# Causal scores in late columns and early quadrants, one weight split moved to GpSimd, and a half-width first level of the inverse

## The reference

```
S = S * w_t[:, :, None, :] + sa[..., None] * bb_t[:, :, None, :] + v_t[..., None] * k_t[:, :, None, :]
y_t = jnp.einsum('bhvk,bhk->bhv', S, r_t)     # sa = S @ aa_t, aa = -kk, bb = kk * a
```

## Time and profile before

| | us |
|---|---|
| median of 3 runs | 1025.52 |
| lowest, highest | 1024.86, 1025.6 |
| profiled execution: its own time | 1025.08 |
| profiled execution: span of its instructions | 1023.1 |

### The profile page before, as it was taken

How to read it: one execution, slowest core, us unless ns; L and a number is a source line. 1 busy time by engine, 2 the same in 40 slices (tenths; PEclk the granted TensorE clock), 3 DMA queues, 4 the chain that set the end, 5 groups by cost and what they waited for, 6 DMA issues and landing times.

```text
span 1023.1 us, 18706 instructions
## 1 busy us (share of the span) xinstructions
PE 1010.8 (99%) x7098; PEld 806.0 (79%) x7098; DVE 736.5 (72%) x1233; ACT 516.5 (50%) x869; POOL 218.1 (21%) x290
## 2 busy tenths in 40 slices
PE   8999999999999999999999999999999999999997
PEld 7888888777777777777777888888888888888886
DVE  5224667788988988888877455367777777789786
ACT  6435766844445445345453322265455444467744
POOL 8532356230221312313210454000000000000000
PEclk9999999999999999999999999999999999999999
DMA  7874465331303313214356877613333333337653
GB/s 201 240 218 139 130 215 203 92 77 42 87 24 73 87 63 86 56 63 119 95 161 149 242 233 255 204 37 102 88 103 90 96 101 103 90 115 221 207 186 117
DMA packets 161291, 133.25 MB, mean 130 GB/s; under 512 B 32730, under 2 KB 137736, under 8 KB 161224
## 3 DMA queue, kind: packets, MB, share of 16 engines
q1 hardware_dynamic: 147552, 88.37, 29.8%
q0 software_dynamic: 13520, 43.90, 13.9%
q10 hardware_dynamic: 151, 0.04, 0.0%
HBM read 111.83 MB, written 20.45 MB: 129 GB/s over the span
## 4 chain that ended last, share of the span: by engine, by line
PE 94%; DVE 2%; ACT 1%; issue 1%; DMA 1%; POOL 0%; ACTq 0%; POOLq 0%; DVEq 0%
PE ps L2075 15%; PE ps L2078 14%; PE ps L2077 14%; PE ps L2031 6%; PE ps L2033 5%; PE ps L2032 5%; PE ps L2634 3%; PE ps L2632 3%; PE ps L2633 3%; PE ps L2247 3%; PE ps L2380 2%; PE ps L2188 2%; PE ps L2567 1%; PE ps L2568 1%; PE ps L2566 1%; PE ps L2329 1%
## 5 line engine op out<-in xcount | busy, mean ns | idle before, releaser
L1340 DVE TENSOR_TENSOR wlo<-raw,whi 128x1024 fp32r<-128x1024 f32 x106 | 138.8, 1310 | 131.6 <-ACT whi L874 113.7
L874 ACT ACTIVATE whi<-raw 128x1024 fp32r<-128x1024 f32 x116 | 122.6, 1057 | 129.7 <-PE ps L2078 117.6
L2075 PE MATMUL ps<-xnh,whi 128*128 128x512 f32 x336 | 130.7, 389 | 0.0
L2077 PE MATMUL ps<-xnl,whi 128*128 128x512 f32 x336 | 130.7, 389 | 0.0
L2078 PE MATMUL ps<-xnh,wlo 128*128 128x512 f32 x336 | 130.7, 389 | 0.0
L2075 PE MATMUL ps<-xh,whi 128*128 128x512 f32 x232 | 91.5, 394 | 1.0 <-DVE xl L1358 1.0
L2077 PE MATMUL ps<-xl,whi 128*128 128x512 f32 x232 | 90.4, 390 | 0.0
L2078 PE MATMUL ps<-xh,wlo 128*128 128x512 f32 x232 | 90.3, 389 | 0.0
L2031 PE MATMUL ps<-xh,whi 128*128 128x512 f32 x192 | 89.5, 466 | 0.0
L2033 PE MATMUL ps<-xh,wlo 128*128 128x512 f32 x192 | 76.0, 396 | 0.0
L2032 PE MATMUL ps<-xl,whi 128*128 128x512 f32 x192 | 75.3, 392 | 0.0
(11 more groups left out here) (424 smaller groups left out, 2434.4 us busy)
## 6 DMA issues: line engine op xcount, KB each, us to landing
raw<-in_w_in SPq DMA_DIRECT2D x108, 256.0 KB, 3.2
raw<-in_w_up SPq DMA_DIRECT2D x88, 256.0 KB, 3.0
wrow<-in_w_down POOLq DMA_DIRECT2D x22, 512.0 KB, 5.3
raw<-weight_scratch SPq DMA_DIRECT2D x44, 256.0 KB, 3.4
raw<-in_w_down SPq DMA_DIRECT2D x32, 256.0 KB, 3.0
weight_scratch<-wrow POOLq DMA_DIRECT2D x11, 512.0 KB, 3.1
gates_scratch<-gst POOLq DMA_DIRECT2D x16, 256.0 KB, 3.3
raw<-in_w_proj_b SPq DMA_DIRECT2D x16, 256.0 KB, 4.0
```

The lines of the kernel that those rows point to most:

```text
L874: act.activation(flat(whi[:, hb]), flat(raw[:, b]), ACT.Copy).then_inc(w_hi, 1)
L1340: dve.tensor_tensor(flat(lo[:, hb]), flat(raw[:, b]), flat(hi[:, hb]).bitcast(F32), ALU.subtract).then_inc(w_lo, 1)
L2075: pe.matmul(ps[bank][:, :], whi[:, hb, k, :], hi(k), start=first and k == 0, stop=False)
L2077: pe.matmul(ps[bank][:, :], whi[:, hb, k, :], lo(k), start=False, stop=False)
```

## The change

- The scores of a pair are computed in three parts. *Late columns*: all 128 rows of a chunk against tokens 64 to 127 of both blocks of `ar`, for `bp`, then for `kp`, a bank to each operand and head. *Early quadrants*, between these: rows 0 to 63 against tokens 0 to 63, for both operands and all chunks; a chunk of odd number goes to partitions 64 to 127 of the bank of its head. The quadrant left out (late rows, early columns) is zero by the mask. No bank is used twice.
- There are still eight masks: two late ones for `gb`, four early ones (64 partitions, four chunks each, both operands), two late ones for `gk`. For that `gb` and `gk` become halves of one tensor `gg`.
- `n1` waits for six masks; the value tokens for one, `bp` for two, `kp` for six.
- The low weights of the first tile of pairs 1 to 7 go from VectorE to GpSimd, as `low_weights`, ahead of `bonus_product`. VectorE waits for them before the first half of the next tile.
- The first product of Y has its even columns alone, as have its two VectorE steps; GpSimd writes the odd columns (`odd_columns`, of the identity) after `bonus_product` and the store behind it, and TensorE waits for them at level 1.

The diff, cut to its core:

```diff
-SCORE_BANK = (0, 1, 2, 3, 4, 5, 0, 1)
+LATE_BANK = ((2, 3), (4, 5))
+EARLY_BANK = (0, 1)
...
+        gg = take("gg", [P, NT, 2, 2, 2, C])
+        gb, gk = (gg[:, 2 * i:2 * i + 2].rearrange("p x e h q t -> p (x e) h (q t)")
+                  for i in range(2))
...
+            def odd_columns(n):
+
+                pool.wait_ge(ops_ready, n + 1)
+                odd = high_half(ident16[:, :], 0).unsqueeze(1).to_broadcast([P, 2 * NT, C // 2, 1])
+                pool.tensor_copy(high_half(yy[:, :, :, :].rearrange("p j h t -> p (j h t)"), 0)
+                                 .rearrange("p (u x) c -> p u x c", x=C // 2), odd)\
+                    .then_inc(odd_set, 1)
...
+            def low_weights(n):
+
+                pool.wait_ge(w_hi, n + 1)
+                pool.wait_ge(w_lo, n)
+                pool.tensor_tensor(flat(wlo[:, n % HL]), flat(raw[:, slot(n)]),
+                                   flat(whi[:, n % HL]).bitcast(F32), ALU.subtract).then_inc(w_lo, 1)
...
             bonus_product(0)
+            odd_columns(0)
...
+                low_weights(N_FILL + 3 * n)
                 bonus_product(n)
                 if 3 * n - 1 >= FILL_V:
                     gate_out(3 * n - 1 - FILL_V)
+                odd_columns(n)
                 remainder(n)
...
             def score_copy(n):
-                act.wait_ge(g_ready, n * 8 + 4)
+                act.wait_ge(g_ready, n * 8 + 6)
...
+            def late_masked(n, i, h):
+                f = 6 * i + h
                 if n == 0:
+                    dve.wait_ge(cleared, 1 + i)
                 dve.wait_ge(g_ps, n * 8 + f + 1)
+                predicated((gb, gk)[i][:, :, h, :].rearrange("p j (q t) -> p j q t", q=2)
+                           [:, :, :, C // 2:], two_parts(causal[:, :], slice(C // 2, C)),
+                           ps[LATE_BANK[i][h]][:, :].rearrange("p (j q t) -> p j q t", j=NT, q=2), f)
+
+            def early_masked(n, h, e):
+                if n == 0:
+                    dve.wait_ge(cleared, 2)
+                dve.wait_ge(g_ps, n * 8 + 6)
+                predicated(gg[0:HD, :, e, h, :, 0:C // 2],
+                           two_parts(causal[0:HD, :], slice(0, C // 2)),
+                           ps[EARLY_BANK[h]][e * HD:(e + 1) * HD, :]
+                           .rearrange("p (x q t) -> p x q t", x=NT, q=2), 2 + 2 * h + e)
...
                         if lv == 0:
-                            yg = yy[:, 2 * g:2 * g + 2].rearrange("p j h t -> p (j h) t")
-                            mask = level_mask[:, 0, :].unsqueeze(1).to_broadcast([P, 4, C])
-                            dve.tensor_tensor(yg, ps[2 * g][:, :].rearrange("p (u t) -> p u t", t=C),
-                                              mask, ALU.mult).then_inc(y_start, 1)
-                            continue
+                            vg = yy[:, 2 * g:2 * g + 2].rearrange("p j h t -> p (j h t)")
...
                     if lv in (1, 2):
+                        if lv == 1 and n:
+                            dve.wait_ge(w_lo, N_FILL + 3 * n + 1)
                         weights_half(N_FILL + 3 * n + 1, lv - 1)
...
-                weights(N_FILL + 3 * n)
                 fill_low(3 * n - 1)
-                for f in range(6):
-                    masked(n, f)
+                masked(n, 0)
                 deviations(n - 1)
-                for f in range(6, 8):
-                    masked(n, f)
+                for i in range(1, 3):
+                    masked(n, i)
...
+                late(0)
+                for i, src in enumerate((bp, kp)):
+                    for jj in range(2):
+                        o = (2 * i + jj) * C
+                        for e in range(2):
+                            j = 2 * jj + e
+                            for h, hs in enumerate(rows):
+                                ins = pe.matmul(ps[EARLY_BANK[h]][e * HD:(e + 1) * HD, o:o + C]
+                                                .rearrange("p (q t) -> p q t", q=2),
+                                                src[hs, j * C:j * C + HD], both(hs, j, slice(0, HD)),
+                                                start=True, stop=True)
+                                if i and jj:
+                                    ins.then_inc(g_ps, 1)
+                late(1)
...
                             else:
-                                ins = pe.matmul(o, n1[:, j, h, :], ident16[:, :], start=True,
-                                                stop=True)
+                                ins = pe.matmul(low_half(o, 0), n1[:, j, h, :],
+                                                low_half(ident16[:, :], 0), start=True, stop=True)
```

More of the change, by code:

```diff
@@ L274, in build @@
         take = taker(KVR, PREP)
-        gb = take("gb", [P, NT, 2, 2 * C])
+        gg = take("gg", [P, NT, 2, 2, 2, C])
+        gb, gk = (gg[:, 2 * i:2 * i + 2].rearrange("p x e h q t -> p (x e) h (q t)")
+                  for i in range(2))
         gst = take("gst", [P, 2, T])
@@ L278, in build @@
         ysb = take("ysb", [P, T])
-        gk = take("gk", [P, NT, 2, 2 * C])
         rkcols = take("rkcols", [P, P // NT])
@@ L399, in build @@
         g_ready = sem("g_ready")
+        odd_set = sem("odd_set")
         tok_ps = sem("tok_ps")
@@ L1502, in deviations, with two_parts, predicated, masked @@
                 spread(ysq, ystd).then_inc(vex_ready, 1)
-            def masked(n, f):
-                j0, h = (f % 4) // 2 * 2, f % 2
-                dst = (gb, gk)[f // 4][:, j0:j0 + 2, h, :]
+            def two_parts(t, ts):
+                return t.rearrange("p (q t) -> p q t", q=2)[:, :, ts]
+            def predicated(dst, mask, scores, f):
+                dve.memset(carrier[:, f:f + 1], 0.0)
+                dve.copy_predicated(dst, mask.bitcast(U32).unsqueeze(1)
+                                    .to_broadcast([mask.shape[0], NT, 2, C // 2]), scores)\
+                    .then_inc(g_ready, 1)
+            def late_masked(n, i, h):
+                f = 6 * i + h
                 if n == 0:
-                    dve.wait_ge(cleared, 1 + f // 4)
+                    dve.wait_ge(cleared, 1 + i)
                 dve.wait_ge(g_ps, n * 8 + f + 1)
[L1512 to L1516, removed]
+                predicated((gb, gk)[i][:, :, h, :].rearrange("p j (q t) -> p j q t", q=2)
[9 more added lines that the diff above has]
+                           .rearrange("p (x q t) -> p x q t", x=NT, q=2), 2 + 2 * h + e)
+            def masked(n, i):
+                if i:
+                    late_masked(n, 1, i - 1)
+                    return
+                for h in range(2):
+                    late_masked(n, 0, h)
+                for h in range(2):
+                    for e in range(2):
+                        early_masked(n, h, e)
             def add_bonus(d):
@@ L1582, in invert @@
                         dve.tensor_tensor(by_unit[0], by_unit[1], mask, ALU.mult)\
-                            .then_inc(v_ready, 1)
+                            .then_inc(v_ready if lv else y_start, 1)
                     if lv == 6:
@@ L1701, in _ @@
             weights(n + 2)
-            for f in range(8):
-                masked(0, f)
+            for i in range(3):
+                masked(0, i)
             value_tokens(0)
@@ L2239, in scores, with both, late @@
                     pe.wait_ge(ps_free, N_FILL - 1)
[L2240 to L2249, removed]
+                rows = [slice(h * HD, (h + 1) * HD) for h in range(2)]
+                def both(hs, j, ts):
+                    return ar[hs, 1 - n % 2, j, :].rearrange("p (q t) -> p q t", q=2)[:, :, ts]
+                def late(i):
+                    src = (bp, kp)[i]
+                    for j in range(NT):
+                        for h, hs in enumerate(rows):
+                            ins = pe.matmul(ps[LATE_BANK[i][h]][:, j * C:(j + 1) * C]
+                                            .rearrange("p (q t) -> p q t", q=2),
+                                            src[hs, j * C:(j + 1) * C], both(hs, j, slice(HD, C)),
                                             start=True, stop=True)
-                            if j > j0:
+                            if j == NT - 1:
                                 ins.then_inc(g_ps, 1)
+                late(0)
+                for i, src in enumerate((bp, kp)):
+                    for jj in range(2):
+                        o = (2 * i + jj) * C
+                        for e in range(2):
+                            j = 2 * jj + e
+                            for h, hs in enumerate(rows):
+                                ins = pe.matmul(ps[EARLY_BANK[h]][e * HD:(e + 1) * HD, o:o + C]
+                                                .rearrange("p (q t) -> p q t", q=2),
+                                                src[hs, j * C:j * C + HD], both(hs, j, slice(0, HD)),
[3 more added lines that the diff above has]
+                late(1)
                 if d is not None:
@@ L2257, in scores @@
                     turned_var(d)
```

(7 more changed lines are left out.)

## The result

The changed kernel takes 1028.8 us (median of 7 executions, 1028.37 to 1029.65); the kernel before, on the same chip, 1025.25 (1024.86 to 1025.6, 7 executions). The ratio is 1.0037, 95% interval [1.0027, 1.0047]: slower, by 3.6 us. The forecast was 1025.5 (1021.7 to 1029.5). The measured time lies inside that range, but the likeliest answer, no change that can be measured, was wrong.

The account below looks back on a forecast made before the run. TensorE and VectorE were taken to bound the seam in turn; +2.0 (pairs 3 to 7), +1.4 (pairs 1 and 2), -0.5 (pair 0) and -2.9 (scans) summed to 0.0, giving 1025.5 us, range 1021.7 to 1029.5.

Parts of the forecast that it names:

- no change that can be measured: Whole kernel: time within 0.2%, 2.05 us, of the kernel before; chance 0.48.
- the distance of the early masks: VectorE at the seam: early masks start 0.70 us apart, between 0.64 and 0.76, so `ysq` is turned at S+6.00.
- the stretch from `ysq` to level 1: TensorE at the seam: from turning `ysq` to level 1 takes 4.09 us instead of 4.42.
- the hold is long: Rival, scan: GpSimd's low weights take 2.8 us, seven scans cost 5.9 instead of 2.9: 1028.5 us; chance 0.16.
- Scan: Seven scans: GpSimd's low weights hold VectorE's `kmod`, TensorE stands still 0.42 us each: -2.9 us.
- early masks one at a time: Rival, VectorE at seams: each early mask starts only after the last ends, 1.7 us more: 1027.2; chance 0.13.
- The eight products go from 0.62 to 0.41, minus 0.21: First level of Y on TensorE, each seam: halving the columns shortens the eight products by 0.21 us.
- the wait ahead of `kp`: TensorE at the seam: its 0.12 us wait before turning `kp` goes, as that turn needs the early masks alone.
- pairs 3 to 7: Seams of these pairs: level 1 at S+10.09 instead of S+10.49, 0.40 us each, +2.0 us (0.8 to 3.2).
- Pairs 1 and 2: Their seams, formerly at S+10.80, reach level 1 0.71 us sooner each: +1.4 us (0.9 to 1.9).
- Pair 0: Early masks wait for the clearing of `gk`; level 1 at about S+10.7 instead of S+10.21: -0.5 us (-1.0 to -0.2).
- the narrow products start 0.03 us apart: Early quadrant scores on TensorE: 32 products about 0.03 us apart, four at a time, take 0.93 us.

Follow-up runs that it names:

- e5: Changed kernel with early masks ordered by partitions, GpSimd's low weights after the pair's operands, and pair 0's clearing of `gk` ahead of the last attention DMA: 1024.65 us.
- e8: Kernel before with only the late columns, early quadrants and their masks: 1028.56 us, ratio 1.0035.
- e2: Changed kernel with the low weights back on VectorE at their old place: 1026.43 us, ratio 1.0014.
- e1: Changed kernel with the early masks reordered, both heads from partition 0, then both from partition 64: 1026.84 us, ratio 1.0019.
- e4: Changed kernel with all four early masks reading partitions 0 to 63, which changes the output: 1024.53 us, ratio 0.9994.
- e13: Changed kernel with the first products of Y writing 64 adjoining columns of PSUM: 1028.24 us, ratio 1.0035.
- e9: Kernel before with only the even-column first level, its products reading 64 adjoining columns of a copied identity: 1024.78 us, ratio 0.9996.
- e10: Kernel before with only the even-column first level, its products writing 64 adjoining columns of PSUM: 1023.44 us, ratio 0.9986.
- e3: Changed kernel with GpSimd's low weights also waiting for the pair's operands, so they run beside the masks: 1026.01 us, ratio 1.0011.

## Why the prediction was wrong

Two steps failed, both in the seam: the distance of the early masks, and the stretch from `ysq` to level 1. That the time came out beside the rival "the hold is long" (1028.5) is chance: its condition, an operation of over 2.67 us on GpSimd, did not come.

**Scan: right.** Forecast 2.38 us for GpSimd's operation, `kmod` 0.72 late, 0.42 a scan; measured 2.36, 0.69 and 0.41 to 0.54 (pair 2 apart). The estimate of 2.25 us from the Trainium skill (GPSIMD Engine Reference, section Elementwise — side-by-side cycle accounting) is 5% short of the 2.36 here. That the second of two operations waits for the other's end was read from two rows of before, and held: `kmod`, `xx` in e5 and the low half in e8 each ended some 0.55 us after GpSimd's operation. The other way round, GpSimd's product (L739) takes 1.27 us in the changed kernel and 2.12 in e2, where it starts beside VectorE's low weights.

**Masks: the first failing step.** The prediction took "the middle, 0.70" for the distance of early masks; it is 0.77. That put `ysq` at S+6.27 where 6.00 was forecast: the mechanism was that of the rival "early masks one at a time", which had a chance of 0.13. The cause, a change of the partition from which the source is read, is shown by e1 (fewer changes) and e4 (none). It is the rule of the Trainium skill (VectorE: DVE Perf Modes, § Two Vector instructions with no wait between them); the trace agrees, 0.76 to 0.78 against 0.63. The middle between two ends was no estimate: each end was a mechanism, either they overlap or they don't, and in this order, where every early mask is followed by a change of partitions, nothing could give 0.70. And what stands behind the same masks besides `ysq`, the value rows `vp` that the first products wait for, was left out of that rival's price.

**First level: the second failing step.** "The eight products go from 0.62 to 0.41, minus 0.21" came from level 1's row of as many columns. The row was of the wrong kind: its write goes in pairs of columns, the new one in single ones. From `ysq` to level 1 it was 4.27 us instead of 4.09. Of the two terms in that step, the wait ahead of `kp` did go (1.19 to `kp` instead of 1.32); the 0.21 didn't come, and the wait for `vp` inside the products added 0.06. The stride was only part of it: in e13, where the write is packed, 0.08 came back, because the second four products wait for `vp`, and the prediction's path to level 1 left that wait out. So pairs 3 to 7 lost 0.09 each instead of gaining 0.40: a miss of 2.45 us, some 0.28 a seam ahead of the turn of `ysq` and some 0.2 behind it.

**Pairs 1 and 2** share both steps: +0.43 instead of +1.4. All that they gained is the weights' op off VectorE.

**Pair 0** was forecast at -0.5 and lost 0.84. The place was right (six masks behind the clearing, then `xx` held by the remainder), the size wrong by the masks' hold.

Sum of the misses: 2.45 for pairs 3 to 7, 0.97 for pairs 1 and 2, 0.34 for pair 0, 0.76 for the scans (0.42 of it the late store) and 0.32 ahead of pair 0 are the 4.84 us of the profiled span. That no change was forecast came from setting a gain that rested on two rows of another kind against a loss that was well founded. Two slips in the working changed nothing: with GpSimd's operation at 2.8 us `kmod` would be 1.14 us late and not 1.26, and the narrow products start 0.03 us apart by the start of the group behind them (0.24 for eight), not by the 0.42 less 0.27.

## What to carry to other kernels

An estimate from a row must match it in everything that the new instruction changes, also in the stride of what it writes and the partition at which it reads, not only in its number of columns. Where two ends of a price are two mechanisms, take one or the other with its chance, never the middle. And an operation moved to GpSimd is free or dear by what VectorE runs beside it: here nothing beside masks from PSUM, 0.4 us a time beside an operation on two tensors of SBUF.

## What the runs showed of the hardware

- Products of 64 columns that write single fp32 columns of PSUM with a gap after each started about every 0.056 us, like products of 128 adjoining ones; with pairs of columns, or 64 adjoining ones, every 0.030. Reading every second fp16 column cost nothing (e9, e10).
- A mask whose source starts in the other half of PSUM's partitions started 0.76 to 0.78 us after the last one instead of 0.63, its own 0.74 plus 0.02 to 0.04 (changed kernel, e1, e4).
- The 32 rows of fp32 quadrant products (64 x 64, two stretches of 64 columns) took 1.03 us. Two at a time they would take 16 x 0.107 = 1.7 us by the kernel before (0.215 us for a couple of twice the columns), four at a time 0.86; so they ran four at a time.
- Beside a GpSimd operation on tensors of SBUF, VectorE's operations on two tensors of SBUF were held until some 0.55 us after its end: 0.68 us became 1.37 (`kmod`), 1.69 (low half, e8), 2.55 (`xx`, e5). Masks from PSUM kept their 0.74 (e3).
- Coming earlier can mean ending later: in e5 `xx` started 0.93 us sooner after the scores than in the changed kernel (S+8.29 instead of S+9.22), met GpSimd's remainder at its start, took 2.55 us instead of 1.24 and ended 0.38 later.
